# The group norm's root, reciprocal and products moved behind the state-space scan

## What is computed

```
def ssd_mixer(xbc, dt_raw, z, h0, dt_bias, a_log, d_skip, g_norm, pad_front, chunk):
    ...
    y, h_last = ssd_scan(padt(xs), padt(dt), A, padt(Bm), padt(Cm), h0g, chunk)
    y = y[:, pad_front:pad_front + T] + d_skip... * xs
    y = y.reshape(b, T, D_INNER) * jax.nn.silu(z.astype(f32))
    yg = y.reshape(b, T, SSD_GROUPS, D_INNER // SSD_GROUPS)
    yg = yg * lax.rsqrt(jnp.mean(yg * yg, axis=-1, keepdims=True) + EPS)
    y = yg.reshape(b, T, D_INNER) * g_norm.astype(f32)
    ...
mixed = jax.nn.sigmoid(ga) * (attn @ w_attn_out) + jax.nn.sigmoid(gs) * (ssd @ w_ssd_out)
```

## Time and profile before

| | us |
|---|---|
| median of 3 runs | 3835.44 (3835.09 to 3847.16) |
| the profiled execution | 3837.69 |
| its span | 3835.9 |
| TensorE busy | 3587.8 (94%) |
| VectorE busy | 2044.3 (53%) |
| ScalarE busy | 809.6 (21%) |
| GpSimd busy | 1537.0 (40%) |

### The profile page before, as it was taken

One profiled execution on the slowest core, in us unless ns is written; L12 is line 12 of the kernel. 1 busy time (PEld: TensorE's weight loads), 2 busy tenths in 40 slices (PEclk: granted clock), 3 DMA queues, 4 the chain that ended last, 5 costly groups with the idle time before them and its releaser, 6 DMA issues.

```text
span 3835.9 us, 57113 instructions
## 1 busy us (share of the span) xinstructions
PE 3587.8 (94%) x22341; PEld 3396.3 (89%) x22341; DVE 2044.3 (53%) x3192; ACT 809.6 (21%) x1626; POOL 1537.0 (40%) x678
## 2 busy tenths in 40 slices
PE   4999999998999999998789989988999899999998
PEld 3999999988978999998688857668999799999998
DVE  3333333355758999977456543894155433433334
ACT  2000000012231111333565323663210200000000
POOL 1453353522323444443286003774443245344351
PEclk8999999999989999999699876999999999999999
DMA  3111111112212222222532124673332011111111
GB/s 68 45 55 44 38 57 36 49 39 73 59 34 64 91 94 93 84 88 76 48 111 78 46 61 115 183 182 109 100 117 93 28 47 57 40 42 57 33 55 55
DMA packets 422192, 272.32 MB, mean 71 GB/s; under 512 B 84342, under 2 KB 397870, under 8 KB 422068
## 3 DMA queue, kind: packets, MB, share of 16 engines
q1 hardware_dynamic: 379352, 225.74, 21.7%
q10 hardware_dynamic: 42716, 44.96, 3.4%
HBM read 211.04 MB, written 59.81 MB: 71 GB/s over the span
## 4 chain that ended last, share of the span: by engine, by line
PE 74%; DVE 15%; ACT 3%; issue 2%; DMA 2%; SPq 2%; ACTq 1%; POOL 1%; another core or an unknown queue 0%; DVEq 0%; POOLq 0%
PE setA L349 8%; PE setA L350 8%; PE setA L351 8%; PE setB L349 7%; PE setB L350 7%; PE setB L351 7%; DVE sc L1064 5%; DVE top L1062 5%; PE bankC L349 2%; PE bankC L351 2%; PE bankC L350 2%; PE bankD L351 2%; PE bankD L349 2%; PE bankD L350 2%; PE bankC L1398 2%
## 5 line engine op out<-in xcount | busy, mean ns | idle before, releaser
L341 POOL TENSOR_TENSOR whi<-wraw,ones 128x1024 fp32r<-128x1024 f32 x192 | 464.1, 2417 | 1723.6 <-PE setA L351 1106.9
L349 PE MATMUL setA<-hhi,whi 128*128 128x352 f32 (+1 forms) x2304 | 756.8, 328 | 45.5 <-issue 15.0
L350 PE MATMUL setA<-hlo,whi 128*128 128x352 f32 (+1 forms) x2304 | 749.4, 325 | 0.0
L351 PE MATMUL setA<-hhi,wlo 128*128 128x352 f32 (+1 forms) x2304 | 748.2, 325 | 0.0
L349 PE MATMUL setB<-hhi,whi 128*128 128x352 f32 (+1 forms) x2304 | 747.4, 324 | 0.0
L350 PE MATMUL setB<-hlo,whi 128*128 128x352 f32 (+1 forms) x2304 | 743.5, 323 | 0.0
L351 PE MATMUL setB<-hhi,wlo 128*128 128x352 f32 (+1 forms) x2304 | 742.3, 322 | 0.0
L349 PEld LDWEIGHTS setA<-hhi,whi 128*128 128x128 f32 x2304 | 439.6, 191 | 54.7 <-issue 25.8
L344 POOL TENSOR_TENSOR wlo<-wraw,whi 128x1024 fp32r<-128x1024 f32 x192 | 474.9, 2473 | 15.1
L350 PEld LDWEIGHTS setA<-hlo,whi 128*128 128x128 f32 x2304 | 439.4, 191 | 2.0
L351 PEld LDWEIGHTS setA<-hhi,wlo 128*128 128x128 f32 x2304 | 439.1, 191 | 0.0
(11 more groups left out here) (405 smaller groups left out, 5841.1 us busy)
## 6 DMA issues: line engine op xcount, KB each, us to landing
wraw<-in_w_in SPq DMA_DIRECT2D x64, 512.0 KB, 3.7
wraw<-in_w_ffn_gate SPq DMA_DIRECT2D x44, 512.0 KB, 3.8
wraw<-in_w_ffn_up SPq DMA_DIRECT2D x44, 512.0 KB, 3.8
wraw<-in_w_ffn_down SPq DMA_DIRECT2D x44, 512.0 KB, 3.5
abc<-acsD SPq DMA_DIRECT2D x8, 2048.0 KB, 9.9
xcD<-cv ACTq DMA_DIRECT2D x24, 520.0 KB, 2.7
xc<-xcD SPq DMA_DIRECT2D x8, 1536.0 KB, 14.5
zD<-spill ACTq DMA_DIRECT2D x16, 524.0 KB, 2.7
```

What stands on the lines that cost most here:

```text
L341: pool.tensor_tensor(dst_cols(slot, hi), dst_cols(slot), ones[:, :].unsqueeze(1).to_broadcast([P, KD, P]), ALU.mult).then_inc(w_hi, 1)
L349: pe.matmul(out, w1, r1, start=start, stop=False)
L350: pe.matmul(out, w1, r2, start=False, stop=False)
L351: return pe.matmul(out, w2, r1, start=False, stop=stop)
```

## The change

- z has a semaphore of its own, `z_loaded`, on which only the gate waits. The gate writes its product over z, in `zc`; `y2` and `ss4` are gone.
- SyncE's order for a chunk (`turn`) is: wait for the last gate, load `abc`, `xc` and `tc` of the chunk after next into the slot, store the undivided rows from `zc` to `sD`, wait for the squares and for that store, load z.
- ScalarE copies each group's sums into one array `sums` of 4 x 1048 columns for all tokens; its loop over chunks is written out, since the columns have fixed addresses. Root, reciprocal and products leave the loop. Behind the scan ScalarE takes two roots of 2 x 1048 columns, and VectorE two reciprocals, ahead of the copies of the final state. The sample rows are stored undivided as well.
- `dve_rows` multiplies the rows in `sraw` by `gssd` and the reciprocal in 24 instructions for each half, as soon as the half is loaded. High and low parts are then made of whole thirds in one instruction each (`act_high`, `dve_low_part`).
- The second load of `sraw` comes behind the second `w_ssd_out` tile's load, not the fourth, and the first gates are loaded two tiles later.

```
         def sp_ssd(sp):
...
+            def turn(c, slot, used, nxt):
+
+                sp.wait_ge(y2_ready, c * SG + SG)
+                if nxt is not None:
+                    load_in(nxt, slot)
+                    load_tok(nxt, slot)
+                store_rows(c, slot)
+                if nxt is not None:
+                    sp.wait_ge(ysq_ready, c * SG + SG)
+                    sp.wait_ge(slot_out[slot], used * 16 + (SSD_OUT1 + 16))
+                    load_z(nxt, slot)
...
-            sp.wait_ge(smp_norm, 1)
+            sp.wait_ge(ysr_ready, 1)
             sp.dma_start(sD.rearrange("(b p) t -> p b t", p=P)[:, :, L:T], ys[:, :, :]).then_inc(bc_stored, 16)
...
+            turn(0, 0, 0, 2)
             with sp.Fori(0, (NCH - 3) // 2) as i:
...
+                turn(i * 2 + 1, 1, i, i * 2 + 3)
+                turn(i * 2 + 2, 0, i + 1, i * 2 + 4)
+            turn(NCH - 2, 1, 0, None)
+            turn(NCH - 1, 0, 0, None)
             load_ao(sp, 2)
...
-                    pe.wait_ge(chunk_loaded[slot], used * 64 + 64)
+                    pe.wait_ge(chunk_loaded[slot], used * 48 + 48)
...
-                act.activation(ss4[:, slot, g, 0:w], bankD[:, 0:w], ACT.Identity).then_inc(ssq_copied, 1)
-                if g == SG - 1:
-                    act.wait_ge(ssq_copied, c * 4 + 4)
-                    act.activation(ss4[:, slot, :, 0:w], ss4[:, slot, :, 0:w], ACT.Sqrt, bias=eps[:, 0:1],
-                                   scale=1.0 / GW).then_inc(root_done, 1)
+                o, _ = tok0(c)
+                act.activation(sums[:, g, o:o + w], bankD[:, 0:w], ACT.Identity).then_inc(ssq_copied, 1)
...
+            act.wait_ge(ssq_copied, 4 * NCH)
+            act.wait_ge(rss_in, 1)
+            for h, dst in enumerate((sums[:, 0:2, :], rs23[:, :, :])):
+                act.activation(dst, sums[:, 2 * h:2 * h + 2, :], ACT.Sqrt, bias=eps[:, 0:1], scale=1.0 / GW)\
+                    .then_inc(root_done, 1)
...
-                if g == 0 and not (isinstance(c, int) and c < 2):
-                    v.wait_ge(slot_out[slot], used * 16 + SSD_OUT1)
+                if g == 0:
+                    v.wait_ge(z_loaded[slot], used * 16 + 16)
...
-            def norm(c, slot):
...
-            norm(NCH - 1, 0)
+            for h, t_ in enumerate((sums[:, 0:2, :], rs23[:, :, :])):
+                v.wait_ge(root_done, h + 1)
+                v.reciprocal(t_, t_).then_inc(rstd_ready, 1)
+            v.wait_ge(slot_out[1], Y_OUT0[1])
             for m in range(NXB // 4):
...
                 load_tile(sp, TILE_SO + m, 0, m % 2, col_tile(so[0:D, :], m * P))
-                if m == 3:
+                if m == 1:
                     sp.wait_ge(part_ready, 6)
...
+        def dve_rows(v, s):
+
+            r = sums if s == 1 else rs23
+            v.wait_ge(rstd_ready, s)
+            v.wait_ge(sraw_loaded, 16 * s)
             for c, (o, w) in enumerate(CH):
...
                 for k in range(KD):
                     b = KD * (s - 1) + k
...
+                    ins = v.scalar_tensor_tensor(sraw[:, k, o:o + w], sraw[:, k, o:o + w], gssd[:, b:b + 1],
+                                                 r[:, k // GB, o:o + w], ALU.mult, ALU.mult)
+                ins.then_inc(rows_ready, 1)
```

More of the change, by code:

```diff
@@ L1801, in build @@
         abc = [at("abc0", [P, SH, P], F32, ABC0), at("abc1", [P, SH, P], F32, BASE)]
[L1802 to L1806, removed]
+        zc = at("zc", [P, 2, NXB, P], F32, mboff + DI * 4)
+        sums = at("sums", [P, SG, T], F32, mboff + DI * 4 + 2 * NXB * P * 4)
         es = at("es", [P, 2, HG, P], F32, WHI)
         ce = at("ce", [P, 2, HG, P], F32, WHI + 2 * HG * P * 4)
+        a = Region(AR, dtT_off - 1024 - AR)
         xdt = a.take("xdt", [P, 2, GW])
@@ L1821, in build @@
          hc_done, h_added, y2_ready, ysq_ready, ssq_done, ssq_copied, small_ready, small_exp, root_done,
-         rstd_ready, norm_ready) = (sem("ssd_" + n) for n in (
+         rstd_ready, rss_in) = (sem("ssd_" + n) for n in (
              "front", "seg", "seg_exp", "ce_exp", "ce", "xdt", "m", "xw", "y", "state", "h_decayed", "h_added",
-             "y2", "ysq", "ssq", "ssq_copied", "small", "small_exp", "root", "rstd", "normed"))
+             "y2", "ysq", "ssq", "ssq_copied", "small", "small_exp", "root", "rstd", "sample_sums"))
         Y_OUT0 = [SSD_OUT1 + 16 * (NCH // 2 + 1 + NXB // 4), SSD_OUT1 + 16 * (NCH // 2)]
@@ L1887, in sp_ssd @@
             phase_over(sp, 1)
[L1888 to L1890 removed]
+            load_tok(0, 0)
+            load_z(0, 0)
+            load_in(1, 1)
+            load_tok(1, 1)
+            load_z(1, 1)
+            sp.wait_ge(ysr_ready, 1)
             sp.dma_start(sD.rearrange("(b p) t -> p b t", p=P)[:, :, L:T], ys[:, :, :]).then_inc(bc_stored, 16)
@@ L2008, in exps @@
                 if g == 0:
-                    act.wait_ge(chunk_loaded[slot], used * 64 + 64)
+                    act.wait_ge(chunk_loaded[slot], used * 48 + 48)
                     act.activation(cd[:, slot, :], abc[slot][:, :, w - 1], ACT.Exp)
@@ L2059, in part_high @@
                 act.activation(hhi[:, :, o:o + w], qT[:, :, o:o + w], ACT.Identity).then_inc(part_hi, 1)
+            act.activation(sums[:, :, L:T], rss[:, :, :], ACT.Identity).then_inc(rss_in, 1)
             exps(0, 0, 0, 0)
-            over_chunks(act, step)
+            for c in range(NCH):
+                step(c, c % 2, c // 2, c + 1 if c < NCH - 1 else None)
             part_high(2, 4 * NCH)
@@ L2105, in seg @@
                 if g == 0:
-                    v.wait_ge(chunk_loaded[slot], used * 64 + 64)
+                    v.wait_ge(chunk_loaded[slot], used * 48 + 48)
                     v.tensor_tensor(ed[0:w, slot, :], abc[slot][0:w, :, w - 1], tc[0:w, slot, SH:2 * SH],
@@ L2171, in step @@
                         weights(n[0], n[1], ns)
-                    if g == 2 and not (isinstance(c, int) and c == 0):
-                        norm(c - 1, 1 - slot)
             v.wait_ge(hT_zero, 1)
@@ L2340, in act_tail @@
                     evac(dst, s, KD - 1, c)
-                    act_high_scaled(act, s + 1, c)
+                    act_high(act, s + 1, sraw, c)
             for m in range(1, KD):
@@ L2361, in dve_tail @@
         def dve_tail(v, ch):
-            dve_part_scaled(v, 1, sraw)
-            dve_part_scaled(v, 2, sraw)
+            for s in (1, 2):
+                dve_rows(v, s)
+                for c in range(3):
+                    dve_low_part(v, s, sraw, c)
             def mix(m, c):
```

89 lines of the change are left out of this document (24 added, 65 removed).

## The result

| | before | after |
|---|---|---|
| median, us | 3841.3 (3835.09 to 3847.2, 4 runs) | 3803.05 (3799.46 to 3809.84, 4 runs) |
| profiled execution, us | 3837.69 | 3799.46 |
| its span | 3835.9 | 3797.7 |

The ratio is 0.9908, with an interval of 0.9894 to 0.9922: faster, by 30 to 41 us. A repetition beside the experiments gave 0.9917 (0.9896 to 0.9937).

The account below looks back on a forecast made before the run. TensorE should need 26.3 us a chunk, but waiting for loads, z last, made it 30.97. Terms 26.7 + 1 + 8.5 - 10 + 10 - 5 = 31.2 off 3835.4 gave 3804 us, range 3790 to 3822.

Parts of the forecast that it names:

- The scan: Chunk loop: with z's wait and the norm gone, the period falls to TensorE's 26.3 us; gain 26.7, bounds 13 and 30.
- Chunk 0: Start of the chunk loop: the first chunk no longer waits for its z, 0 to 2 us, taken as gain 1.
- The added chain: Chunk loop: rows' store, then z's reload, puts z in place at t0 + 25.5, hidden under compute by 6 us.
- The cover of `tc`: Chunk loop: without z, the `tc` load lands about 0.9 us before TensorE's front is due.
- The end of the scan: Last state product to the attention tiles: norm gone and some clock regained; gain 8.5 us, bounds 5 and 11.
- Behind the scan: Final state: two wide VectorE reciprocals ahead of its copies make TensorE wait; loss 10 us, bounds 7 and 13.
- thinnest cover: Fifth attention tile: weights queued behind the state's stores are ready at S + 58, as the tile before ends; counted 0.
- The seams: Two seams between parts of the products: rows scaled ahead, thirds in single passes; gain 10 us, bounds 6 and 11.
- The second row load: Third `w_ssd_out` tile: its weights come late behind the earlier 4 MB `sraw` load; loss 5 us, bounds 1 and 8.
- The second rival: Behind the scan: GpSimd passes at seams, a split behind row products and late `load_ao(4)` cost more; 3816, chance 0.17.
- The third rival: Chunk loop stays paced by transfers: `tc` 2 us later returns half the stall, 14 us less gain; 3818, chance 0.12.
- The fifth: Chunk loop: rows' store and z's reload become the loop, deciding from z at t0 + 33; 3849, chance 0.04.

Follow-up runs that it names:

- The kernel with z apart: The kernel before with z on its own semaphore, on which only the gate waits, norm and root kept in the loop: 3836.76 us, ratio 0.999.
- The kernel with wide parts alone: The kernel before with each third's high and low part made in one instruction each, gain `gssd` left out: 3825.61 us, ratio 0.9965.

## Why the prediction held, point by point

The mechanism held, and every term but the scan's came out within two microseconds. That the median lies 1 us from 3804 is luck: the sum had 31.2 us of gain, taken off the 3835.4 of three runs; the gain measured is 38.3, against a kernel before whose four runs have a median of 3841.3. A sum too small by 7 met a base too low by 6.

*The scan, 26.7 and 1 forecast, 31.4 measured.* The step from the stall to the gain was right: both z's wait and the norm had to go, since the norm "would be the next bound". One sentence of it was not: that the norm "is hidden there". It outlasted z's landing by 1.1 us and held the chunk together with it. The kernel with z apart shows that this bound alone keeps the whole 31 us, and the kernel without reciprocal and products shows the period drop with it. The term was mis-sized in three small ways: the six stalls gave 25.0 in five periods and 4.9 behind the last `abc` issue, 5.0 each for 4.7 (1.7 more); the period ahead of them, which the sum took to be free, gave 1.4 in this pair of traces (30.61 before, 29.19 after, but 30.78 in the repetition of after, so this part is scatter); and the 1.5 kept back for late loads was not lost. The 31.4 lies 1.4 above the bound of 30. Chunk 0, counted at 1, lies ahead of the stretch, where executions scatter too much to read it.

*The added chain*, store then reload, was forecast to put z in place 25.5 us behind the `abc` issue. The rows give 20.0 + 5.6 = 25.6: the store took 7.5 instead of 5.4, and the reload was issued as soon as the store had landed. The next `abc` was issued 0.7 behind z's landing (0.8 forecast). The cover of `tc`, called 0.9, is as thin as it was said: 4.1 us of lateness brought 5.0 a chunk. The kernel where the front waits for z shows what hides the chain: its consumer, the gate, lies five groups later.

*The end of the scan, 8.5 forecast.* The step to the first product gave 8.3 (7.3 forecast, since no GpSimd pass stood in the way of the first low part). It stood in the way of the second and third: two passes of 5.23 and 5.12 us beside two low parts that together took 9.79, and two waits of 0.91 and 0.99. The clock that the prediction counted on did come back: the granted clock is 1.00 from the first product on, where before it was 0.50 from there to 2630, some 2.5 us of loss. But the slower second and third low parts ate it: from the first product to the last eviction of the third tile it took 38.94 us, before 38.97. So the 1.2 of this term was not won, and the end of the scan gave 8.3.

*Behind the scan, a loss of 10 forecast.* Reciprocals of 13.25 and 13.19 (13.4 forecast), a wait of 6.83 (7.5), an eviction gap of 13.76 where 4.73 is normal: 9.0 (8.4 in the repetition). Putting the copies ahead of the second reciprocal gave that back, less 1.4 at the next wait. The "thinnest cover", tile 5's weights, held: the first pass of its split starts at 2633.82 behind the landing, and no pause of TensorE follows.

*The seams, 10 forecast.* Two tiles took 2701.64 - 2678.61 = 23.03 at the first, 5.4 less than in the earlier trace rows. The 1 us kept back for a GpSimd pass was not needed. The second gave 4.7 (in the last line of the ledger) and 0.7 at the tile ahead of it, whose evictions no longer lie 4.2 us apart: 10.8 in all. The kernel with wide parts alone gives 8 to 19, which holds the 11 but does not sharpen it.

*The second row load, a loss of 5 forecast.* 10.38 - 3.85 = 6.5, inside the bounds of 1 and 8; undoing it gave 7.4 at that place.

*Not forecast:* 1.5 us where GpSimd's pass took 10.12 us (5.40 between two evictions instead of 3.85). The second rival, row products in the way of splits, was right in kind; its price was this one place, and in the repetition nothing.

Against the ledger, whose -10.9 is 5.4 and 0.7 less 9.0, 6.5 and 1.5: 31.4 + 8.3 - 10.9 + 6.2 = 35.0 where the sum had 31.2; the rest of the 38.2 lies ahead of the scan, where the executions scatter. The surplus is the scan's.

The third rival (2 us of `tc` lateness, 14 us) did not come about, but the store put first showed the mechanism and made it dearer than priced: about 4 us late cost 23 to 27. The fifth (store and reload become the loop) stayed far off: z at 25.6 of the 33 where it would decide.

## What to carry to other kernels

When an engine stalls on a load, look for what other work runs inside that stall: here the norm filled it and ended a microsecond behind it, and taking away either alone gave 0.2 or 1.1 us of the 5. Work taken out of a loop lands somewhere, and its place there, ahead of or behind a copy that others wait for, decided 8 or 9 of its microseconds. On one queue, put the small load that the next step waits for ahead of the large store whose landing is needed only later.

## What the runs showed of the hardware

**A pause can cost more than its length.** After the wait of 6.83 us in after, the granted clock (behind GpSimd's busy time) was at 0.50, the 1.2 GHz level, until 2632, and then back at 2.4 GHz:

```profile
2616.00:2620.00 4.00, 4.00 (x27) 4.00 (x26) 4.00 (x1) 0.47 (x1) 0.00 (x0) 1.00 0.00 0
2628.00:2630.00 2.00, 2.00 (x9) 2.00 (x10) 1.23 (x3) 0.00 (x0) 0.00 (x0) 0.50 0.56 158
...
2631.00:2632.00 1.00, 1.00 (x5) 1.00 (x4) 0.00 (x0) 0.00 (x0) 0.00 (x0) 0.50 0.93 268
...
2634.00:2638.00 4.00, 4.00 (x27) 4.00 (x26) 0.00 (x0) 0.46 (x1) 3.92 (x2) 1.00 0.84 214
```

What such a pause costs beyond its wait is the time between evictions less the usual time and the wait. It was 2.2 us on 6.83 here, but 1.5 on the same 6.83 in the repetition, where the clock was back some 1.3 us sooner, and 2.8 with the store first; ahead of the third `w_ssd_out` tile it was 1.6 on 4.94 here and 2.7 on 6.10 with the copies first. In the scan with the front waiting for z, the five periods hold 42.1 us in which TensorE is not busy and 12.0 us more of busy time than the five of after, at a mean granted clock of 0.87, so 8.4 and 2.4 a period:

```profile
2416.17:2601.79 185.62, 143.53 (x1142) 107.97 (x1141) 101.28 (x146) 85.32 (x232) 118.04 (x61) 0.87 0.61 157
```

It is no fixed toll. In the kernel before, the clock was at 0.55 behind the wait of 2.88 us at 2455.49, and at 1.00 behind one of 3.06 us at 2516.13 (and behind one of 2.03 us at 2485.61):

```profile
2458.00:2460.00 2.00, 2.00 (x14) 1.45 (x12) 2.00 (x5) 2.00 (x8) 1.95 (x1) 0.55 1.01 291
2517.00:2528.00 11.00, 10.82 (x98) 8.11 (x97) 10.68 (x16) 6.61 (x18) 7.87 (x4) 1.00 0.34 95
```

In the prediction the stall of 4.7 us was read off as a whole, so this did not hurt; in the expectation for the front that waits for z it did.

**A run of short VectorE instructions can hold GpSimd out for as long as the run.** In after the pass of 10.12 us lies beside 24 row products (2650.14 to 2662.07, 0.57 to 0.59 us each); without them it takes 2.40. The next pass starts 10.20 us behind its start, so it is no error of the recorded end alone. But in the repetition of the same kernel the pass got in after 3.2 us of the run and took 2.58, and VectorE paid: one product took up to 2.72 us, and the 24 of them 16.21 instead of 11.93.

```profile
2661.77 16.21 DVE L2293 SCALAR_TENSOR_TENSOR sraw<-sraw,gssd,sums 128x352 f32<-128x352 f32 x24 [19.60 <-DMA sraw<-sD]
2665.00 2.58 POOL L341 TENSOR_TENSOR whi<-wraw,ones 128x1024 fp32r<-128x1024 f32 x1 [6.62 <-PE setA L351]
```

Of seven traces with these products, three show the long pass (10.12, 10.18 and 10.62 us) and four the long run. The Trainium skill (SBUF — State Buffer, Who interferes with whom) says that a VectorE instruction with two SBUF inputs contends with a GpSimd instruction that reads SBUF, under an exclusive lock, and that the order of issue decides who blocks. The trace agrees that one waits for the other. What it adds is that the loser can wait for a whole run of instructions and not only for one, and no run here shows what decides between the two outcomes.

**A wide reciprocal is dear**: 13.25 us for 2096 columns, twice the 6.69 of 1048 in the earlier trace rows (on 32 partitions), so 6.3 ns a column, against 1.0 ns a column for ScalarE's root (2.05 us for 2096).
